# Output bias of the banded attention layers: from one-row products on TensorE to an addition into the residual on GpSimd

## The chip, the cores and the metric

The kernel runs on one core of a Trainium2 chip, in one launch. The metric is device time in microseconds. All times below come from hardware runs of it.

## The reference, cut to what matters

A first block (a token mixer with three branches, then a mixture of 16 experts) yields x, 256 tokens by 1024 features. Four post-norm transformer layers follow, and the change lies in two of them:

```python
for i in range(4):
    kind, j = i % 3, i // 3
    if kind == 0:   # layers 0 and 3: banded ("sliding window") attention
        h = mixer_a(x, a_w_qkv[j], a_b_qkv[j], a_sinks[j], a_w_o[j], a_b_o[j], cos, sin)
    elif kind == 1:
        h = mixer_b(x, b_w_qkv[j], b_w_o[j], cos, sin)
    else:
        h = mixer_c(x, c_w_qkv[j], c_w_o[j], cos, sin)
    x = layer_norm(DN_ALPHA * x + h, ln_g[i, 0], ln_b[i, 0])
    x = layer_norm(DN_ALPHA * x + swiglu(x, w_gate_up[i], w_down[i]), ln_g[i, 1], ln_b[i, 1])
```

`mixer_a` ends in `o.reshape(B, S, nq) @ w_o + b_o`: it alone has an output bias, `b_o`, one row of 1024 values that is the same for every token. DN_ALPHA is 8 to the power 1/4.

## The kernel before, in words

Each engine runs a program of its own; semaphores order them. Weights stream from HBM as units of 128x1024 values into a ring of 12 (SyncE's queue, L351). ScalarE rounds each unit into `high` (L1185), VectorE subtracts to get `low` (L1660), and every product of two fp32 operands is made of three: high by high, high by low, low by high. In the four layers all products run through the helper at L443. The residual x lies in SBUF as two tiles of 128 tokens by 1024; LayerNorm rewrites it in place (L2005, L2006), TensorE transposes it (`turn`, L531, counted in `x_turned`) and ScalarE and VectorE write its transposed halves `xs`, which the projections read.

A banded layer (`kind == 0`) treats its 16 heads as four quads q0 to q0+3. TensorE's order is written out by hand: projections of values, keys and the four quads' queries, the scores of each quad in between, then `weighted_values(q0)` and `weighted_values(q0+1)` (transposes of the weights at L1052 to L1054, then a gather into `pg`), then the output projection. ScalarE copies a gathered quad out as `oth` (L1559), VectorE subtracts for `otl` (L2215), counted in `otl_out`.

The output projection accumulates into the four banks of `pd`, one for each half of the features of each token tile. Before its first real product TensorE waits for `bo_landed` and opens each bank with a product of a row of ones by a row of the bias (L1131, both fp32, so each is recorded as two matmuls), and the last of them gives `bo_used`. `wo_part(n, t)` then adds the products with weight unit n: units 0 to 3 for both token tiles first, 48 products of 128x512 in all, behind `otl_out` of quad q0+1; then quad q0+2's values, units 4 and 5, quad q0+3's values, and the rest. VectorE's `residual(t, h)` reads a bank, computes ALPHA times x plus the bank in one instruction (L1966) and takes its statistics (L1970); LayerNorm follows, whose gain is `gb[:, 0]` and whose bias is `gb[:, 1]`.

GpSimd's queue, in the second half of the kernel, does two things. At the end of each LayerNorm it loads the rows for the next (L426 to L433), spread over all partitions: in front of a banded layer `a_bo` goes to `gb[:, 0]` (L428) and `ln_b` to `gb[:, 1]` (L429). `attention(layer)` then multiplies the exponentials of each quad by the reciprocals of their sums (`weigh`, L369), each behind VectorE's `recip`; between the third and the fourth quad of a banded layer it waits for `bo_used` and loads `ln_g` over the bias (L380). Nothing else is in its queue.

Of the kernel before, what the change touches and what calls it, by code (L numbers as in the profile page):

```python
# [22 lines left out]
ALU = mybir.AluOpType  # L23
# [4 lines left out]
KT = D // P  # L28
T = 256
TT = T // P  # L30
# [12 lines left out]
ALPHA = (2 * LAYERS) ** 0.25  # L43
# [74 lines left out]
def build_program(nc, a, out):  # L118
# [7 lines left out]
    with ExitStack() as ctx:  # L126
# [17 lines left out]
        ones = sb("ones", [P, P])  # L144
# [8 lines left out]
        gb = sb("gb", [P, 2, D])  # L153
# [45 lines left out]
        pd = pb("pd", [P, 4, 512])  # L199
# [14 lines left out]
        x = rs[:, 2048:4096].rearrange("p (t d) -> p t d", t=TT)  # L214
# [78 lines left out]
        def S(name):  # L293
            if name not in sems:
                sems[name] = ctx.enter_context(nc.semaphore(name))
            return sems[name]
# [24 lines left out]
        def row_of(name):  # L321

            o = D * LONG.index(name)
            return a["long_rows"][o:o + D].partition_broadcast(P)
# [35 lines left out]
        def _(gp):  # L360
# [12 lines left out]
            def attention(layer):  # L373

                kind, q0 = KINDS[layer], 4 * layer
                for i in range(3):
                    weigh(q0 + i)
                if kind == 0:
                    gp.wait_ge(S("bo_used"), layer // 3 + 1)
                    gp.dma_start(gb[:, 0, :], row_of(f"ln_g{2 * layer}")).then_inc(S("gains_landed"), 16)  # L380
                weigh(q0 + 3)

            gp.memset(cs[:, :, :], 0.0).then_inc(S("cs_zero"), 1)
# [40 lines left out]
            for n in range(3, 3 + 2 * LAYERS):  # L424
                layer = (n - 3) // 2
# [13 lines left out]
        def _(pe):  # L439
            held = [""]  # L440

            def mm(dst, lhs, rhs, start, stop, skip=False):
                ins = nc.tensor.matmul(dst, lhs, rhs, start=start, stop=stop, skip_group_check=skip)  # L443
                if held[0]:
                    ins.then_inc(S(held[0]), 1)
                    held[0] = ""
                return ins
# [131 lines left out]
            for k in range(KT):  # L579
                g = k % 4  # L580
                last = mm(pm[0][32 * g:32 * g + 32, :], wg32[:, k, :], hc[:, :, k, :], k < 4, k >= 4)
# [3 lines left out]
            for s in range(4):  # L585
                last = mm(pm[0][:, s * 16:(s + 1) * 16], gate_rows[:, s * P:(s + 1) * P], fold[:, 0:16], True, True)
# [7 lines left out]
            for r, dst in ((0, pm[1]), (1, pm[0])):  # L594
                for j in range(4):
                    fwd, bwd = (2, 3, 0, 1)[j], (3, 2, 1, 0)[j]
                    mm(dst[0:8, j * P:(j + 1) * P], zp[:, r, fwd, :], ident, True, False)
                    last = mm(dst[0:8, j * P:(j + 1) * P], zp[:, 2 + r, bwd, :], flip, False, True)
# [5 lines left out]
            for i in range(4):  # L604
                last = mm(pm[1][:, (4 + i) * 8:(5 + i) * 8], rr_of[(4, 0)[i // 2]][:, (2 + i % 2) * P:(3 + i % 2) * P],
                          ident[0:8, 0:8], True, True)
# [81 lines left out]
            for h in range(MLH):  # L688
                for t in range(2):
                    last = nc.tensor.transpose(pd[:, h // 2, (h % 2) * T + t * P:(h % 2) * T + (t + 1) * P],  # L690
                                               hml[:, t, h, :], ident)
# [386 lines left out]
            for layer, kind in enumerate(KINDS):  # L1078
# [45 lines left out]

                n0 = first[("wo", layer)]
                pe.wait_ge(S("masked"), PROJ[q0 + 4])
                if kind == 0:
                    pe.wait_ge(S("bo_landed"), 16 * (layer // 3 + 1))
                    for t in range(TT):
                        for c in range(2):  # L1130
                            last = mm(pd[:, 2 * t + c, :], ones[0:1, :], gb[0:1, 0, c * 512:(c + 1) * 512], True, False)  # L1131
                    last.then_inc(S("bo_used"), 1)

                def wo_part(n, t):
                    w = weights(n0 + n)
                    i, c = n // 2, n % 2
                    for k in (2 * i, 2 * i + 1):
                        for l, r in ((0, 0), (0, 1), (1, 0)):
                            o = (k % 2) * 512
                            last = mm(pd[:, 2 * t + c, :], (oth, otl)[l][:, k, t * P:(t + 1) * P], w[r][:, o:o + 512],  # L1140
                                      kind > 0 and k == 0 and (l, r) == (0, 0), k == KT - 1 and l == 1)
                    return last

                pe.wait_ge(S("otl_out"), q0 + 2)
# [483 lines left out]
        def _(dve):  # L1628
# [326 lines left out]
                then(V.tensor_tensor(mix[:, m, :], mix[:, m, :], mtmp[:, 0, :], ALU.add))  # L1955
                V.tensor_tensor(mix[:, m, :], mix[:, m, :], mtmp[:, 1, :], ALU.add).then_inc(S("mixed"), 1)

            def residual(t, h, mod=None):

                half = x[:, t, h * 512:(h + 1) * 512]  # L1960
                src = pd[:, 2 * t + h, :]
                if mod is not None:
                    then(V.tensor_tensor(rtmp, src, gb[:, mod, h * 512:(h + 1) * 512], ALU.mult))
                    ins = V.tensor_tensor(half, half, rtmp, ALU.add)
                else:
                    ins = V.scalar_tensor_tensor(half, half, ALPHA, src, ALU.mult, ALU.add)  # L1966
                ins.then_inc(S("res_out"), 1)
                RES[0] += 1
                dve.wait_ge(S("res_out"), RES[0])
                V.bn_stats(n_stats[:, t, h, :], half).then_inc(S("vector_step"), 1)  # L1970
                steps[0] += 1
# [247 lines left out]
            for layer, kind in enumerate(KINDS):  # L2219
# [72 lines left out]
                low_output(q0 + 3)  # L2292
                split_to(w0 + 11)
                n = 3 + 2 * layer
                for h in range(2):
                    dve.wait_ge(S("wo_first"), 2 * layer + h + 1)
                    residual(0, h)
                statistics(n, 0, False)
                normalised(n, 0)
                dve.wait_ge(S("unit_used"), w0 + 8 - split0)  # L2300
                residual(1, 0)
                low_part(n, 0)
                residual(1, 1)
                statistics(n, 1, False)
                normalised(n, 1)
                low_part(n, 1)
# [225 lines left out]
```

## Time and profile before

| | us |
|---|---|
| median of 3 runs (2242.11 to 2250.87) | 2242.16 |
| the profiled execution's own time | 2242.46 |
| its span, first to last instruction | 2240.6 |
| TensorE busy, matmuls | 2110.4 |
| VectorE busy | 1288.6 |
| ScalarE busy | 919.5 |
| GpSimd busy | 109.9 |

In the profile PE is TensorE's matmuls and PEld its weight loads, DVE is VectorE, ACT ScalarE, POOL GpSimd and SP SyncE. Durations in rows are us unless marked ns; a matmul's record is longer than its share of the array, since matmuls overlap, so the pace is read from the distance between two starts. In brackets stands how long the engine was idle before an instruction and what ended that. PEclk is the granted TensorE clock as a share of 2.4 GHz, so 0.50 is 1.2 GHz. Times along the run count from the first instruction. The profiled execution's time is 1.9 us more than its span.

### The profile page before, as it was taken

Reading aid. Unit: us, or ns where it says so; the run is one execution under the profiler, and the core shown is the slowest. Engines: PE = TensorE matmul, PEld = TensorE weight load, DVE = VectorE, ACT = ScalarE, POOL = GpSimd, SP = SyncE. Lnnn points to the kernel's source line nnn. Section 1 sums busy time; section 2 is a strip of 40 time slices with the busy share of each in tenths; the row PEclk is TensorE's granted clock in tenths of the full one; section 3 lists DMA queues with packets and bytes.
Section 4 is the critical chain, followed back from the end, with each engine's and each line's share of the span. In section 5 each row is a group of like instructions: output and inputs, shape, how many; then the busy total and the mean of one; then the engine's idle time right before and its main releaser. Section 6 shows DMA issues by size and latency. Waiting matters only on the chain.

```text
span 2240.6 us, 27821 instructions
## 1 busy us (share of the span) xinstructions
PE 2110.4 (94%) x11438; PEld 1691.7 (75%) x11438; DVE 1288.6 (58%) x1890; ACT 919.5 (41%) x1452; POOL 109.9 (5%) x115
## 2 busy tenths in 40 slices
PE   6999999998999988999999998999998999989997
PEld 2468667856888885788799997788796888867886
DVE  3345723346555575745677875755686655757554
ACT  2233341015444445444435554444364544454442
POOL 1000000000000002000001111000011000020000
PEclk9999999999999999999999999999999999989999
DMA  8142444434555541555453432555443555424541
GB/s 346 46 178 67 186 167 150 178 122 160 187 188 178 181 165 70 188 187 179 168 180 140 162 132 76 196 182 186 169 151 113 203 180 182 168 85 150 187 175 70
DMA packets 47118, 357.36 MB, mean 159 GB/s; under 512 B 5370, under 2 KB 5541, under 8 KB 9680
## 3 DMA queue, kind: packets, MB, share of 16 engines
q1 hardware_dynamic: 41904, 336.61, 41.4%
q0 software_dynamic: 4800, 18.50, 2.4%
q8 instruction: 91, 1.49, 0.3%
q10 hardware_dynamic: 288, 0.47, 0.1%
q14 instruction: 35, 0.29, 0.0%
HBM read 354.51 MB, written 1.05 MB: 159 GB/s over the span
## 4 chain that ended last, share of the span: by engine, by line
PE 85%; DVE 9%; ACT 4%; issue 1%; DMA 1%; POOL 0%; SPq 0%; ACTq 0%; DVEq 0%
PE pg L443 55%; PE pd L443 24%; PE pm L443 3%; PE pm L908 1%; DVE small L1970 1%; DVE rs L2006 1%; DVE rs L2005 1%; DVE rs L1966 1%; DMA ring<-in_wstream 1%; DVE low L1660 1%; PE pm L1052 1%; DVE ar L1764 1%; DVE xs L2016 1%; ACT high L1185 1%; ACT ar L1546 1%
## 5 line engine op out<-in xcount | busy, mean ns | idle before, releaser
L1660 DVE TENSOR_TENSOR low<-ring,high 128x1024 fp32r<-128x1024 f32 x512 | 619.8, 1231 | 372.3 <-ACT high L1185 372.0
L443 PE MATMUL pg<-high,xs 128*128 128x512 f32 (+1 forms) x2496 | 744.1, 375 | 24.1 <-DVE xs L2016 14.3
L1185 ACT CAST high<-ring 128x1024 fp32r<-128x1024 f32 x512 | 525.1, 1049 | 367.7 <-PE pd L443 164.5
L443 PEld LDWEIGHTS pg<-high,xs 128*128 128x128 f32 x2496 | 459.4, 192 | 112.9 <-issue 21.3
L443 PE MATMUL pg<-low,xs 128*128 128x512 f32 (+1 forms) x1248 | 465.0, 373 | 0.0
L443 PE MATMUL pd<-high,hid 128*128 128x512 f32 x960 | 311.9, 396 | 7.0 <-DVE hid L2095 7.0
L443 PEld LDWEIGHTS pg<-low,xs 128*128 128x128 f32 x1248 | 240.0, 192 | 40.5
L443 PE MATMUL pg<-xs,high 128*128 128x256 f32 x1344 | 242.1, 283 | 0.0
L443 PEld LDWEIGHTS pd<-high,hid 128*128 128x128 f32 x960 | 180.6, 188 | 50.9 <-DVE hid L2095 8.2
L443 PEld LDWEIGHTS pg<-xs,high 128*128 128x128 f32 x1344 | 206.2, 188 | 5.3 <-issue 5.0
L443 PE MATMUL pg<-rh,ring 128*128 128x256 f32 (+1 forms) x832 | 204.0, 405 | 0.0
L443 PEld LDWEIGHTS pg<-rh,ring 128*128 128x128 f32 x832 | 160.0, 194 | 42.4 <-issue 22.5
L443 PE MATMUL pd<-low,hid 128*128 128x512 f32 x480 | 189.7, 395 | 0.0
L443 PE MATMUL pg<-xs,low 128*128 128x256 f32 x672 | 189.3, 282 | 0.0
L443 PEld LDWEIGHTS pg<-xs,low 128*128 128x128 f32 x672 | 126.6, 188 | 0.0
L443 PEld LDWEIGHTS pd<-low,hid 128*128 128x128 f32 x480 | 90.3, 188 | 21.3
L369 POOL TENSOR_TENSOR ar<-ar,small 128x256 f32<-128x256 f32 (+1 forms) x64 | 83.7, 1336 | 409.5 <-DVE small L2208 409.5
L2095 DVE TENSOR_TENSOR hid<-pm,hid 128x512 fp32r<-128x512 f32 x60 | 41.4, 691 | 92.6 <-ACT hid L1477 92.6
L1477 ACT CAST hid<-pm 128x512 fp32r<-128x512 f32 x60 | 35.2, 587 | 124.4 <-PE pm L908 124.4
L1486 ACT ACTIVATE ar<-pg 128x256 f32<-128x256 f32 x120 | 46.0, 384 | 84.2 <-PE pg L443 84.1
L1546 ACT ACTIVATE ar<-ar,small 128x257 f32<-128x257 f32 (+5 forms) x128 | 66.9, 526 | 17.6 <-DVE small L2202 9.6
L1764 DVE SCALAR_TENSOR_TENSOR ar<-rs,vecs,ar 128x256 f32<-128x256 f32 x160 | 70.5, 482 | 2.9
(333 smaller groups left out, 1968.4 us busy)
## 6 DMA issues: line engine op xcount, KB each, us to landing
ring<-in_wstream SPq DMA_DIRECT2D x256, 1024.0 KB, 4.8
ring<-in_wstream SPq DMA_DIRECT2D x31, 2048.0 KB, 7.8
gb<-in_long_rows POOLq DMA_DIRECT2D x21, 512.0 KB, 4.5
hdec<-in_hy_decay POOLq DMA_DIRECT2D x4, 512.0 KB, 6.5
rh<-in_xt SPq DMA_DIRECT2D x1, 1024.0 KB, 11.7
rh<-in_ctx SPq DMA_DIRECT2D x1, 1024.0 KB, 20.0
cx<-in_cx_tables POOLq DMA_DIRECT2D x1, 1024.0 KB, 5.1
cx<-in_dft_tables POOLq DMA_DIRECT2D x1, 1024.0 KB, 8.5
```

Of the source, the lines that this page charges most:

```text
L369: last = gp.tensor_tensor(w, w, smx[:, b, 2, t, 2 * p:2 * p + 2].unsqueeze(2).to_broadcast([P, 2, n]), ALU.mult)
L443: ins = nc.tensor.matmul(dst, lhs, rhs, start=start, stop=stop, skip_group_check=skip)
L908: last = nc.tensor.transpose(pm[u % 2][:, i * T + t * P:i * T + (t + 1) * P], hidden[:, t, i * P:(i + 1) * P], ident)
L1052: nc.tensor.transpose(pm[i][:, 0:P], scores(q, 0)[:, h, g * P:(g + 1) * P], ident)
L1185: nc.scalar.copy(high[:, (s - split0) % NHIGH, :], ring[:, s % NRAW, :]).then_inc(S("high_done"), 1)
L1477: nc.scalar.copy(hid[:, u % 2, 0, :, :], pm[u % 2][:, :].rearrange("p (i t) -> p i t", t=T)).then_inc(S("hid_high"), 1)
L1486: nc.scalar.activation(silu_g[:, t, :], pg[t][:, 0:T], ACT.Silu).then_inc(S("silu_done"), 1)
L1546: last = nc.scalar.activation(s, s, ACT.Exp, bias=smx[:, b, 0, t, h:h + 1], accum_out=smx[:, b, 1, t, h:h + 1])
L1660: V.tensor_tensor(low[:, s % NRAW, :], ring[:, s % NRAW, :], high[:, (s - split0) % NHIGH, :].bitcast(F32), ALU.subtract).then_inc(S("low_ ...
L1764: last = V.scalar_tensor_tensor(d, src, w[i], d, ALU.mult, ALU.add)
L1966: ins = V.scalar_tensor_tensor(half, half, ALPHA, src, ALU.mult, ALU.add)
L2095: V.tensor_tensor(hid[:, u % 2, 1, :, :], pm[u % 2][:, :].rearrange("p (i t) -> p i t", t=T), hid[:, u % 2, 0, :, :].bitcast(F32), ALU.sub ...
```

## The change

In the two banded layers GpSimd waits until the bias has landed and x has been transposed, multiplies each tile of x by ALPHA, adds the bias row, and then loads `ln_g` over the bias. It does so ahead of the first quad's weighing. TensorE no longer opens the accumulators with one-row products, and the first real product of each bank overwrites it. VectorE waits for the additions and then adds the bank to x without a factor.

```diff
--- before.py
+++ after.py
@@ -373,11 +373,17 @@
             def attention(layer):
 
                 kind, q0 = KINDS[layer], 4 * layer
+                if kind == 0:
+                    gp.wait_ge(S("bo_landed"), 16 * (layer // 3 + 1))
+                    gp.wait_ge(S("x_turned"), 4 * (2 + 2 * layer))
+                    for t in range(TT):
+                        gp.tensor_scalar(x[:, t, :], x[:, t, :], ALPHA, None, ALU.mult).then_inc(S("x_raised"), 1)
+                        gp.wait_ge(S("x_raised"), 2 * (layer // 3) + t + 1)
+                        gp.tensor_tensor(x[:, t, :], x[:, t, :], gb[:, 0, :], ALU.add).then_inc(S("bo_added"), 1)
+                    gp.wait_ge(S("bo_added"), 2 * (layer // 3 + 1))
+                    gp.dma_start(gb[:, 0, :], row_of(f"ln_g{2 * layer}")).then_inc(S("gains_landed"), 16)
                 for i in range(3):
                     weigh(q0 + i)
-                if kind == 0:
-                    gp.wait_ge(S("bo_used"), layer // 3 + 1)
-                    gp.dma_start(gb[:, 0, :], row_of(f"ln_g{2 * layer}")).then_inc(S("gains_landed"), 16)
                 weigh(q0 + 3)
 
             gp.memset(cs[:, :, :], 0.0).then_inc(S("cs_zero"), 1)
@@ -1124,12 +1130,6 @@
 
                 n0 = first[("wo", layer)]
                 pe.wait_ge(S("masked"), PROJ[q0 + 4])
-                if kind == 0:
-                    pe.wait_ge(S("bo_landed"), 16 * (layer // 3 + 1))
-                    for t in range(TT):
-                        for c in range(2):
-                            last = mm(pd[:, 2 * t + c, :], ones[0:1, :], gb[0:1, 0, c * 512:(c + 1) * 512], True, False)
-                    last.then_inc(S("bo_used"), 1)
 
                 def wo_part(n, t):
                     w = weights(n0 + n)
@@ -1138,7 +1138,7 @@
                         for l, r in ((0, 0), (0, 1), (1, 0)):
                             o = (k % 2) * 512
                             last = mm(pd[:, 2 * t + c, :], (oth, otl)[l][:, k, t * P:(t + 1) * P], w[r][:, o:o + 512],
-                                      kind > 0 and k == 0 and (l, r) == (0, 0), k == KT - 1 and l == 1)
+                                      k == 0 and (l, r) == (0, 0), k == KT - 1 and l == 1)
                     return last
 
                 pe.wait_ge(S("otl_out"), q0 + 2)
@@ -1955,13 +1955,15 @@
                 then(V.tensor_tensor(mix[:, m, :], mix[:, m, :], mtmp[:, 0, :], ALU.add))
                 V.tensor_tensor(mix[:, m, :], mix[:, m, :], mtmp[:, 1, :], ALU.add).then_inc(S("mixed"), 1)
 
-            def residual(t, h, mod=None):
+            def residual(t, h, mod=None, raised=False):
 
                 half = x[:, t, h * 512:(h + 1) * 512]
                 src = pd[:, 2 * t + h, :]
                 if mod is not None:
                     then(V.tensor_tensor(rtmp, src, gb[:, mod, h * 512:(h + 1) * 512], ALU.mult))
                     ins = V.tensor_tensor(half, half, rtmp, ALU.add)
+                elif raised:
+                    ins = V.tensor_tensor(half, half, src, ALU.add)
                 else:
                     ins = V.scalar_tensor_tensor(half, half, ALPHA, src, ALU.mult, ALU.add)
                 ins.then_inc(S("res_out"), 1)
@@ -2292,15 +2294,17 @@
                 low_output(q0 + 3)
                 split_to(w0 + 11)
                 n = 3 + 2 * layer
+                if kind == 0:
+                    dve.wait_ge(S("bo_added"), 2 * (layer // 3 + 1))
                 for h in range(2):
                     dve.wait_ge(S("wo_first"), 2 * layer + h + 1)
-                    residual(0, h)
+                    residual(0, h, None, kind == 0)
                 statistics(n, 0, False)
                 normalised(n, 0)
                 dve.wait_ge(S("unit_used"), w0 + 8 - split0)
-                residual(1, 0)
+                residual(1, 0, None, kind == 0)
                 low_part(n, 0)
-                residual(1, 1)
+                residual(1, 1, None, kind == 0)
                 statistics(n, 1, False)
                 normalised(n, 1)
                 low_part(n, 1)
```

## Rows read from the trace of the kernel before

**Rows 1.** The page: busy time by engine; the chain that ended last.

```profile
PE 2110.4 (94%) x11438; PEld 1691.7 (75%) x11438; DVE 1288.6 (58%) x1890; ACT 919.5 (41%) x1452; POOL 109.9 (5%) x115
...
PE 85%; DVE 9%; ACT 4%; issue 1%; DMA 1%; POOL 0%; SPq 0%; ACTq 0%; DVEq 0%
```

**Rows 2.** Uses of tile gb, whole run: ns min/median/max; DMA issue to landing, us.

```profile
L443 PE MATMUL pd<-gb,ones x16: 587/1009/1218, 862.0 to 1996.3; 1*128 1x512 f32 x16
...
L1963 DVE TENSOR_TENSOR ar<-pd,gb x8: 674/688/692, 483.8 to 800.0; 128x512 f32<-128x512 f32 x8
...
L380 POOL DMA_DIRECT2D gb<-in_long_rows x2: 592/593/594, 866.4 to 1997.6; - x2
...
DMA to landing us min/median/max: 3.8/4.5/7.3
```

**Rows 3.** Timeline, 855 to 885 us, layer 0: start, duration in us, engine, line, operation.

```profile
862.03 4.07 PE L443 MATMUL pd<-gb,ones 1*128 1x512 f32 x8
...
862.77 0.69 DVE L2215 TENSOR_TENSOR otl<-pg,oth 128x512 fp32r<-128x512 f32 x1 [2.25 <-ACT oth L1559]
...
866.03 0.80 PE L443 MATMUL pd<-high,oth 128*128 128x512 f32 x1
...
873.05 0.40 PE L443 MATMUL pd<-high,oth 128*128 128x512 f32 x1
...
873.28 0.39 PE L443 MATMUL pd<-low,oth 128*128 128x512 f32 x1
...
879.99 0.27 PE L1052 MATMUL pm<-consts,ar 128*128 128x128 f32 x1
```

**Rows 4.** The chain that ended last, 880 to 890 us: start, duration in us, what.

```profile
884.14 0.70 DVE otl L2215
...
884.88 3.04 PE pd L443 x12
```

**Rows 5.** Timeline, 1980 to 2014 us, layer 3.

```profile
1990.12 7.19 PE L443 MATMUL pd<-gb,ones 1*128 1x512 f32 x8
...
1990.86 0.69 DVE L2215 TENSOR_TENSOR otl<-pg,oth 128x512 fp32r<-128x512 f32 x1 [3.72 <-ACT oth L1559]
...
1997.24 0.80 PE L443 MATMUL pd<-high,oth 128*128 128x512 f32 x1
...
2010.55 0.27 PE L1052 MATMUL pm<-consts,ar 128*128 128x128 f32 x1
```

**Rows 6.** Stretch, length, busy us of PE, PEld, DVE, ACT, POOL; PEclk, DMA, GB/s.

```profile
809.00:836.00 27.00, 27.00 (x243) 26.05 (x242) 20.82 (x29) 12.62 (x18) 0.00 (x0) 1.00 0.49 176
862.00:865.00 3.00, 3.00 (x9) 1.41 (x8) 2.23 (x3) 2.85 (x12) 1.13 (x2) 1.00 0.00 0
865.50:872.00 6.50, 6.50 (x15) 4.72 (x15) 0.49 (x3) 0.75 (x4) 3.76 (x5) 0.50 0.22 81
882.00:886.00 4.00, 2.59 (x21) 1.82 (x22) 1.61 (x2) 3.03 (x5) 0.00 (x0) 1.00 0.54 229
1985.50:1997.00 11.50, 11.08 (x30) 5.31 (x30) 4.86 (x9) 5.71 (x21) 3.17 (x4) 0.50 0.01 1
1997.00:2001.50 4.50, 4.50 (x11) 3.40 (x11) 0.00 (x0) 0.00 (x0) 3.76 (x5) 0.50 0.35 117
```

**Rows 7.** Timeline of GpSimd, 805 to 850 us; in brackets its idle time before.

```profile
841.97 3.98 POOL L369 TENSOR_TENSOR ar<-ar,small 128x256 f32<-128x256 f32 x4 [35.27 <-DVE small L2208]
```

**Rows 8.** GpSimd's instructions by form, whole run: busy us, mean ns of one.

```profile
L369 POOL TENSOR_TENSOR ar<-ar,small 128x1536 f32<-128x1536 f32 x8 | 24.8, 3102 | 0.0
...
L395 POOL MEMSET rs<- 128x3684 f32 x1 | 3.2, 3169 | 23.0 <-PE pd L443 23.0
```

**Rows 9.** VectorE's residual step, whole run: ns min/median/max.

```profile
L1966 DVE SCALAR_TENSOR_TENSOR rs<-rs,pd x32: 669/680/690, 895.1 to 2231.7; 128x512 f32<-128x512 f32 x32
```

**Rows 10.** Timeline of VectorE, 1965 to 1975 us, layer 3: the rotation's second step.

```profile
1969.66 1.25 DVE L2162 SCALAR_TENSOR_TENSOR ar<-ar,ropes 128x256 f32<-128x256 f32 x1
...
1973.82 0.42 DVE L2162 SCALAR_TENSOR_TENSOR ar<-ar,ropes 128x256 f32<-128x256 f32 x1
```

## The prediction, made before the changed kernel was run

> **What bounds the kernel now.** I read the page first, then every use of the bias rows, then the instructions in order of time around them in both banded layers, then the same stretches with TensorE's granted clock. The page says that TensorE is busy 94% of the span and carries 85% of the chain that ended last [rows 1]. So whatever leaves TensorE's queue without leaving a hole is worth its full duration. The rows on the bias then show 16 records of one-row products, two for each of the 4 accumulators of a layer, at 0.59 us in the one layer and about 1.0 us in the other [rows 2]. In order of time they are one block in each layer: in layer 0 from 862.03 to 866.03 us, where the first full product of the output projection starts [rows 3]; in layer 3 from 1990.12 to 1997.24 us [rows 5]. That is 4.0 and 7.1 us of TensorE for work that fills one row of the array.
>
> **What is late next.** The projection also waits for the low half of the second quad's output (`otl_out`), behind the same gather that TensorE has just finished. VectorE starts that subtraction at 862.77 us, 0.74 us after the block began [rows 3]. At a later hand-over of the same kind, where nothing covers it, TensorE starts 0.74 us after VectorE's start (884.14 to 884.88) [rows 4]. So without the block the first full product starts at 862.77 + 0.74 = 863.51 us, not at 862.03, and the block's removal gives 866.03 - 863.51 = 2.5 us. In layer 3 the same reckoning is 1990.86 + 0.74 = 1991.60, and 1997.24 - 1991.60 = 5.6 us [rows 5]. Together 8.1 us, out of 11.1 us of removed block; 3.0 us come back as an idle wait.
>
> **The clock.** In layer 0 the granted clock is 1.00 during the block (862 to 865) and 0.50, that is 1.2 instead of 2.4 GHz, in the 6.5 us behind it [rows 6]. TensorE was busy without a gap before that fall, and what it had been doing was the one-row block. The 48 full products that follow take 879.99 - 866.03 = 13.96 us, while two of them stand 0.23 us apart at the upper level (873.05, 873.28) [rows 3]; 48 x 0.23 = 11.0, so 2.9 us are lost to the lower level. In layer 3 the clock is 0.50 before and during the block and stays there for 4.5 us of full products behind it [rows 6]; the 48 products take 2010.55 - 1997.24 = 13.3 us [rows 5], a loss of 2.3 us, or 4.6 us of running at half speed.
>
> Would the clock hold in layer 0 after the change? TensorE would gather, idle 1.4 us and start full products. The hand-over of rows 4 is just that, and the stretch around it (882 to 886, TensorE busy 2.59 of 4.00 us) kept 1.00 [rows 6]. So I take the 2.9 us as gained, with bounds 0 and 2.9. In layer 3 the clock is low on arrival. Full products then start after 1.4 us of idling instead of after 7.1 us of one-row products; bounds are a gain of the whole 2.3 us and a loss of as much more; I take half of it gained, 1.1 us, since the trace shows the block unable to raise the clock in 7 us and full products able to in under 5 (those 4.6 us).
>
> The Trainium skill, TensorE: Matmul & The Clock Gate, section What's actually happening, ties the clock to how busy the array has been and does not discount thin products. By that rule the one-row block keeps the clock up and the new idle wait endangers it, so the sum would be 8.1 us or less. Here the trace disagrees: the clock fell under uninterrupted one-row products.
>
> **What is added on GpSimd.** Four passes over 128x1024 per layer: two multiplications by ALPHA, two additions of the bias, each behind its semaphore. The trace has no one-operand arithmetic there. Bounds per element come from the memset (3.17 us for 3684, 0.86 ns) and the widest product with a broadcast (3.10 us for 1536, 2.02 ns) [rows 8]: 0.9 and 2.1 us a pass, 6 to 8.3 us in all; I take 8, as the arithmetic is nearest to the second row. They wait for the bias to land, 4.5 us after its issue and at worst 7.3 [rows 2], and for the last transposes of x. GpSimd's queue is otherwise empty: its first weighing in layer 0 starts at 841.97 us after 35.3 us of idling, released by VectorE's reciprocal [rows 7]; layer 3 repeats this. So the passes run from about 810 to 818 us (813 to 821 at worst), 20 us before anything behind them is wanted. Cost 0; if that cover were gone, the 8 us would go straight into the weighing and the chain.
>
> The gain row (`ln_g`) is now loaded behind the passes at about 818 us, 48 us earlier than now (866.4 [rows 2]); it is one 512 KB transfer, beside weight loads that take half of the DMA time there (0.49 [rows 6]) and run a ring of twelve units ahead. It moves past all of GpSimd's weighing but no weight load waits behind it. Cost 0. GpSimd's fourth weighing no longer waits for `bo_used`; nobody waits for it at that time.
>
> **VectorE.** Its four residual steps per layer turn from a three-operand form (0.680 us) into a plain addition out of PSUM, for which 0.688 us is the nearest row [rows 2, 9]: 8 x 0.008, nothing. The added wait on `bo_added` is met by about 818 us, and the first residual comes behind 884 us. What may cost is sharing: with GpSimd at work the rotation's 128x256 step takes 1.25 instead of 0.42 us [rows 10]. From 809 to 836 us VectorE is busy 20.8 of 27.0 us and TensorE 27.0 of 27.0 [rows 6], so TensorE waits for none of it and VectorE can lose about 6.2 us. If it loses all 8 us of the passes, the excess is 1.8 us a layer. I take 0, because TensorE shows no gap at all there, so no split weight comes just in time.
>
> **Sum.** 2.5 + 2.9 in layer 0, 5.6 + 1.1 in layer 3, together 12.1 us. Everything behind layer 0 runs some 5 us earlier, and the stretches in which TensorE idles meet the clock's changes elsewhere; with the fall of layer 0 priced at 2.9 us, I set aside a quarter of another one, 0.8 us. The profiled execution took 2242.46 us (span 2240.6), 0.3 us over the median 2242.16; it gives 2231.2, and from the median 2242.16 - 11.3 = 2230.9 us.
>
> **Rivals.**
> 1. *The clock does not care what fills the array.* Then only 8.1 us are gained, and the new idle wait can cost another fall in one of the layers, 2.9 us: 2234 to 2237 us. For it: in layer 3 the clock was low before the block. Against it: the fall in layer 0. Chance 0.14; it is what that section's rule would do here.
> 2. *Falls elsewhere.* The block's price is regained but layers 1 to 3 pick up two more falls of about 2 us at the places where TensorE waits: 2235 us, chance 0.12. The opposite is as open: in layer 3, reached earlier, the clock may be up before the products start, as it is in layer 0 (1.00 at 862), which gives 1.2 us more there and spares the low stretch ahead of them, some 4 us in all: 2227 us, chance 0.17.
> 3. *VectorE starved, slower.* The passes on GpSimd run not 2 but 5 us each, and VectorE is held for their length. TensorE then waits for split weights: (20 - 6.2) x 2 = 27.6 us lost against 11.3 gained, 2258 us. It turns into a loss where a layer's passes hold VectorE for more than 6.2 + 5.7 = 12 us. For it: the threefold step of rows 10. Against it: the rates of rows 8. Chance 0.03. The Trainium skill, SBUF — State Buffer, section Who interferes with whom, states that a VectorE instruction with two SBUF inputs and a GpSimd one that reads SBUF block each other for a whole instruction, not by shares; by that rule the loss is at most the passes' own 8 us, 1.8 us a layer after the slack, and the time 2234.5. It speaks against this change, as the splits have two SBUF inputs; the threefold step agrees with it in kind.
> 4. *It does not do what it says.* TensorE, freed of the block, stands at another wait up to the old time: the transposes behind the 48 products, for instance, wait for ScalarE. 2242 us. ScalarE is busy 0.75 of 6.50 us behind the block [rows 6], so 0.03.
>
> The rest, 0.51, is the forecast with its own spread of about 2228.5 to 2233.5. A measurement here can tell about 0.5%, 11.2 us, from no change; the forecast sits on that line, so its cases split. Faster by more: rival 2's good side, 0.17, and a little over half of the forecast's 0.51, in all 0.45. Slower by more: rival 3 with a little for what I have not seen, 0.04. Within: the rest, 0.51. The range leaves out rivals 3 and 4 and the tails: 2226.5 to 2237.
>
> **What would show it.** No records of one-row products into these accumulators. The first full product about 0.74 us behind the start of VectorE's subtraction, with TensorE idle some 1.4 us before it. Granted clock 1.00 in the 48 products of layer 0, which then take 11.0 us. Four GpSimd passes of some 2 us from 4 to 5 us behind the bias's issue, over long before the first reciprocal. VectorE's first splits of the layer up to twice as long, and no new wait of TensorE's there. The forecast is wrong if TensorE's first product is later than that, if the clock falls under the projection in layer 0 as before, or if TensorE waits for a split weight in the first 27 us of a banded layer.

## The result, and the profile after

| | median, us | lowest to highest | runs |
|---|---|---|---|
| before | 2246.54 | 2242.11 to 2250.87 | 7 |
| after | 2234.39 | 2231.93 to 2238.45 | 7 |

The ratio is 0.9947, with a 95% interval from 0.9932 to 0.9963. The changed kernel is faster by 12.2 us where 11.3 were forecast (2242.16 to 2230.9, a ratio of 0.9950). The base moved: of the three runs known beforehand two are the lowest of the seven and one the highest, so that their median, 2242.16, lies 4.4 us under that of all seven. The changed kernel ran once more later, with 12 runs beside 23 of before: 2239.29 against 2248.64 us, 0.9953 [0.994, 0.9966].

The profiled execution of the changed kernel took 2233.47 us (span 2231.7). First the page: busy time by engine, to be held against [rows 1].

```profile
PE 2095.2 (94%) x11422; PEld 1688.4 (76%) x11422; DVE 1298.7 (58%) x1890; ACT 919.6 (41%) x1452; POOL 133.9 (6%) x123
```

TensorE has the 16 records of [rows 2] less and 15.2 us less work. GpSimd has 24.0 us more, VectorE 10.1 us more without one more instruction.

Next the chain that ended last, from the end of the gather to the end of the 48 products. The kernel before in layers 0 and 3 (two windows of the chain, one for each layer: start, duration, what):

```profile
859.50 2.61 PE pg L443 x16
862.10 18.05 PE pd L443 x56
...
1990.19 20.52 PE pd L443 x56
```

The changed kernel:

```profile
859.11 2.76 PE pg L449 x16
861.87 1.46 issue
863.33 12.71 PE pd L449 x48
...
1989.57 1.46 issue
1991.03 11.34 PE pd L449 x48
```

The 56 records (8 thin, 48 full) became an idle wait of 1.46 us and 48 full ones: 18.05 to 14.17 us in layer 0, 20.52 to 12.80 in layer 3, which is 3.9 and 7.7 us.

The wait is for `otl`, as forecast. The profile names no releaser for it ("issue"); the product starts 0.11 us behind the end of VectorE's subtraction, and in e3 below the wait is gone where the first products need only the quad before. The timeline of the changed kernel, VectorE's subtraction and TensorE's first full product in layer 0:

```profile
862.53 0.69 DVE L2217 TENSOR_TENSOR otl<-pg,oth 128x512 fp32r<-128x512 f32 x1 [3.78 <-ACT oth L1559]
...
863.33 0.77 PE L449 MATMUL pd<-high,oth 128*128 128x512 f32 x1 [1.46 <-issue]
```

The clock did not do in layer 0 what was forecast. Stretches of the changed kernel, with the columns of [rows 6] (busy us of PE, PEld, DVE, ACT, POOL; then PEclk, DMA, GB/s):

```profile
809.00:836.00 27.00, 27.00 (x262) 25.72 (x260) 23.69 (x28) 11.87 (x18) 10.32 (x5) 1.00 0.52 181
...
856.50:866.00 9.50, 6.95 (x28) 4.96 (x29) 5.30 (x9) 6.37 (x25) 3.51 (x5) 0.50 0.01 2
866.50:876.00 9.50, 9.50 (x44) 7.67 (x43) 0.00 (x0) 0.00 (x0) 2.34 (x3) 1.00 0.30 110
900.50:903.50 3.00, 3.00 (x8) 2.32 (x8) 2.52 (x9) 0.20 (x1) 0.00 (x0) 0.50 0.26 109
...
1991.00:2002.00 11.00, 10.97 (x48) 8.95 (x49) 2.46 (x4) 2.72 (x12) 3.18 (x4) 1.00 0.26 95
```

It was low (0.50) from before the gather until 866 us, through the new idle wait and the first full products, and 1.00 behind that. In layer 3 the clock was up for all 48 products. A low stretch (0.50 again) has appeared at 900.5 us, where the feed-forward products start. The kernel before at that place in layer 0, and in layer 3, where it has such a stretch too:

```profile
900.00:912.00 12.00, 9.26 (x46) 6.93 (x44) 10.75 (x21) 2.46 (x5) 0.95 (x2) 1.00 0.40 165
2036.00:2039.00 3.00, 3.00 (x9) 2.35 (x8) 2.49 (x9) 0.20 (x1) 0.00 (x0) 0.50 0.00 0
```

Last the passes on GpSimd, by the timeline, layer 0:

```profile
802.39 0.53 POOL L434 DMA_DIRECT2D gb<-in_long_rows  x1 [300.83 <-DVE rs L2005]
...
806.83 3.11 POOL L380 TENSOR_SCALAR rs<-rs 128x1024 f32<-128x1024 f32 x1 [3.39 <-DMA gb<-in_long_rows]
810.03 2.64 POOL L382 TENSOR_TENSOR rs<-rs,gb 128x1024 f32<-128x1024 f32 x1
812.64 3.74 POOL L380 TENSOR_SCALAR rs<-rs 128x1024 f32<-128x1024 f32 x1
816.47 2.41 POOL L382 TENSOR_TENSOR rs<-rs,gb 128x1024 f32<-128x1024 f32 x1
819.18 0.61 POOL L384 DMA_DIRECT2D gb<-in_long_rows  x1 [0.30 <-POOL rs L382]
840.21 3.98 POOL L369 TENSOR_TENSOR ar<-ar,small 128x256 f32<-128x256 f32 x4 [20.42 <-DVE small L2210]
```

They take 806.83 to 818.88, 12.1 us and not 8, and GpSimd then still idles for 20.4 us. VectorE pays for some of it; its timeline, 803 to 830 us (a line with x4 or x2 is that many splits together; two with nothing beside them take 2.35 us):

```profile
804.95 5.47 DVE L1660 TENSOR_TENSOR low<-ring,high 128x1024 fp32r<-128x1024 f32 x4 [0.22 <-ACT high L1185]
...
811.64 4.09 DVE L1660 TENSOR_TENSOR low<-ring,high 128x1024 fp32r<-128x1024 f32 x2 [1.22 <-ACT high L1185]
...
816.83 2.60 DVE L2163 TENSOR_TENSOR ar<-ar,ropes 128x512 f32<-128x512 f32 x1 [1.10 <-ACT ar L1529]
...
823.01 0.69 DVE L2163 TENSOR_TENSOR ar<-ar,ropes 128x512 f32<-128x512 f32 x1
```

Two splits took 4.09 us and a rotation step 2.60 instead of 0.69. TensorE is busy 27.00 of 27.00 us from 809 to 836 all the same.

### The profile page after: what moved, and what is told of

The parts are those of the page before. It is cut to its first block, busy times and chain, and to the rows that moved or that the text cites. A ratio compares the mean times of both kernels' runs of the same rounds, so it can differ in the third digit from the quotient of the medians.

```text
span 2231.7 us, 27799 instructions
## 1 busy us (share of the span) xinstructions
PE 2095.2 (94%) x11422; PEld 1688.4 (76%) x11422; DVE 1298.7 (58%) x1890; ACT 919.6 (41%) x1452; POOL 133.9 (6%) x123
## 4 chain that ended last, share of the span: by engine, by line
PE 85%; DVE 9%; ACT 3%; issue 2%; DMA 1%; POOL 0%; SPq 0%; ACTq 0%; DVEq 0%
PE pg L449 55%; PE pd L449 24%; PE pm L449 2%; PE pm L914 1%; DVE small L1972 1%; DVE rs L2008 1%; DMA ring<-in_wstream 1%; DVE rs L2007 1%; DVE low L1660 1%; PE pm L1058 1%; DVE ar L1764 1%; DVE rs L1968 1%; ACT high L1185 1%; ACT ar L1546 1%; DMA rh<-in_xt 1%
## 5 line engine op out<-in xcount | busy, mean ns | idle before, releaser
L1660 DVE TENSOR_TENSOR low<-ring,high 128x1024 fp32r<-128x1024 f32 x512 | 626.2, 1243 | 370.9 <-ACT high L1185 370.6
```

The costliest lines, as they stand in the source:

```text
L1660: V.tensor_tensor(low[:, s % NRAW, :], ring[:, s % NRAW, :], high[:, (s - split0) % NHIGH, :].bitcast(F32), ALU.subtract).then_inc(S("low_ ...
```

## The experiments

The theory: the gain is the one-row block taken off TensorE's path, part of it by its length and part by the clock, which thin products do not keep up; GpSimd's work costs nothing. The rivals: the gain is in the other edits (a plain addition, an earlier `ln_g`); the clock does not care what fills the array; the passes cost something that the gain hides.

Each ratio below is to the kernel before, measured beside it on the same chip; its interval in brackets is the 95% one. The chips differ, so ratios are compared and not microseconds. Stage times are from the chains that ended last.

### e1: the block gone, and no passes

```diff
-    gp.wait_ge(S("x_turned"), 4 * (2 + 2 * layer))
-    for t in range(TT):
-        gp.tensor_scalar(x[:, t, :], x[:, t, :], ALPHA, None, ALU.mult).then_inc(S("x_raised"), 1)
-        gp.wait_ge(S("x_raised"), 2 * (layer // 3) + t + 1)
-        gp.tensor_tensor(x[:, t, :], x[:, t, :], gb[:, 0, :], ALU.add).then_inc(S("bo_added"), 1)
-    gp.wait_ge(S("bo_added"), 2 * (layer // 3 + 1))
...
-    dve.wait_ge(S("bo_added"), 2 * (layer // 3 + 1))
...
-    residual(0, h, None, kind == 0)
+    residual(0, h)
...
```

The two other calls of `residual` change alike, and the output bias is left out of the result.

> The changed kernel without GpSimd's four passes in each banded layer; VectorE multiplies by ALPHA as before, and the output bias is left out of the result. Theory (the passes are hidden): the same time as the changed kernel, 2234 us within 2 us, TensorE's schedule in the first 27 us of a banded layer unchanged. Rival (VectorE's held splits cost something after all): 2 to 4 us faster than the changed kernel, 2230 to 2232.

Measured: 2238.24 us (5 runs) against 2248.72 (17): 0.9948 [0.9933, 0.9964]. The changed kernel has 0.9947 and 0.9953. So the four passes, the wait on `bo_added` and the plain addition cost nothing that can be measured; the intervals leave room for some 4 us either way, so by the times alone the rival of 2 to 4 us would not be excluded. The traces are sharper: TensorE's waits in front of the gather are the same with the passes and without (more under g1). The expected 2234 us were missed because the kernel before stood at 2248.7 on that chip; the ratio is the one expected.

### e2: the block back, for nothing

The changed kernel with the eight one-row products in front, on a row of other values; the first full products overwrite what they wrote.

```diff
     pe.wait_ge(S("masked"), PROJ[q0 + 4])
+    if kind == 0:
+        for t in range(TT):
+            for c in range(2):
+                mm(pd[:, 2 * t + c, :], ones[0:1, :], cxf[0:1, c * 512:(c + 1) * 512], True, True)
```

> The changed kernel with the eight one-row product records put back in front of the projection in each banded layer (their values are overwritten by the first real product). Theory (the block was the price, by its own length and by the clock falling under it): as slow as the kernel before, 2245 to 2248 us, with the granted clock at one half behind the block. Rival (only the block's length counts): 8 us above the changed kernel, 2242 us, and the clock behind the block no lower than without it. Rival (the gain came from elsewhere): 2234 us.

Measured: 2249.25 us (12 runs), 1.0002 [0.9989, 1.0015]. The block alone takes the whole gain away. Its chain, layer 0 and layer 3:

```profile
862.77 18.05 PE pd L449 x56
...
1994.97 16.89 PE pd L449 x56
```

Layer 0 takes the same 18.05 us as before to the last digit; layer 3 found a higher clock and lost 4.1 us against the changed kernel instead of 7.7. The eight records alone take 3.95 us there (1994.97 to 1998.92) where they took 7.1 in the trace of before: that figure was a matter of where the clock stood on arrival.

### c1 and c2: the block five times, thin and full

Both are made from the kernel before. c1 repeats the one-row products, c2 has the same count, columns and type with all 128 rows (the bias enters the result with another factor there).

c1:

```diff
+    for _ in range(4):
+        mm(pd[:, 2 * t + c, :], ones[0:1, :], gb[0:1, 0, c * 512:(c + 1) * 512], True, True)
     last = mm(pd[:, 2 * t + c, :], ones[0:1, :], gb[0:1, 0, c * 512:(c + 1) * 512], True, False)
```

c2:

```diff
-    last = mm(pd[:, 2 * t + c, :], ones[0:1, :], gb[0:1, 0, c * 512:(c + 1) * 512], True, False)
+    for _ in range(4):
+        mm(pd[:, 2 * t + c, :], ones[:, :], gb[:, 0, c * 512:(c + 1) * 512], True, True)
+    last = mm(pd[:, 2 * t + c, :], mean_w[:, :], gb[:, 0, c * 512:(c + 1) * 512], True, False)
```

> The kernel before with the block of one-row products issued five times over in each banded layer (40 records instead of 8). Theory (one-row products do not keep the clock up): the granted clock falls to one half inside the block and stays there to its end in both layers, wherever it began; a record then takes 0.85 us, the block some 28 to 34 us. Rival (a busy TensorE keeps its clock whatever fills the array): the clock rises within the block and stays, 0.43 us a record, 17 to 20 us.

> The same five-fold block with all 128 rows in each product (all rows of the bias tile are equal, so only the factor of the added bias changes, and the bias in the result is wrong). Theory: the clock is up within about 5 us of the block's start at the latest and stays there into the projection; 0.43 us a record at the upper level, 17 to 20 us a block, and 48 products of 11.0 us behind it. Rival: no difference from the one-row block.

Measured, one run each and so without an interval, before at 2245.66: c1 2299.71, c2 2264.9. That is 54 and 19 us for the same 64 extra records, 0.84 and 0.30 us each (in c2 the records themselves stand 0.41 us apart; the difference is what the other products of the stage gain). c1's chain and its stretches in layer 0:

```profile
864.33 2.76 PE pg L443 x16
867.09 43.89 PE pd L443 x88
```

```profile
867.50:870.00 2.50, 2.50 (x7) 1.10 (x6) 2.25 (x3) 2.50 (x12) 0.00 (x0) 1.00 0.00 0
871.00:898.00 27.00, 27.00 (x32) 9.99 (x30) 0.18 (x1) 0.23 (x2) 0.00 (x0) 0.50 0.00 0
898.00:901.00 3.00, 3.00 (x8) 2.35 (x8) 0.00 (x0) 0.00 (x0) 2.54 (x4) 0.50 0.39 142
902.00:910.00 8.00, 8.00 (x36) 6.49 (x35) 0.00 (x0) 0.00 (x0) 0.22 (x1) 1.00 0.36 132
```

The same of c2:

```profile
862.99 29.07 PE pd L443 x88
```

```profile
858.00:863.00 5.00, 4.28 (x23) 2.90 (x23) 1.89 (x5) 1.91 (x6) 3.17 (x4) 0.50 0.01 3
864.50:880.00 15.50, 15.50 (x38) 6.89 (x37) 2.38 (x4) 2.64 (x12) 0.00 (x0) 1.00 0.00 0
880.00:891.00 11.00, 11.00 (x48) 8.61 (x47) 0.00 (x0) 0.00 (x0) 3.77 (x5) 1.00 0.39 143
```

In c1 TensorE is busy without a gap (27.00 of 27.00 us) and the clock is down for all of it: it was 1.00 half a microsecond behind the block's start (867.5 to 870), 0.50 from 871 us on, and came back only once full products ran, which start at 898.1 us. In c2 the block starts inside a low stretch, the clock is up 1.3 us later (864.2) and stays up. Layer 3 of both runs does the same: 0.50 from 2028 to 2056 us under c1's block, 1.00 from 2007.8 to 2023 under c2's. Count, columns, type and busy share are alike; the rows are not. The Trainium skill, TensorE: Matmul & The Clock Gate, section What's actually happening, says that the clock follows how busy the engine has been. By that alone both blocks would hold it up; c1 shows that a busy engine is not enough when one row of the array is fed.

### e5: the block once, with full rows

The clock's share of the block's price without removing anything: before, with one line of the block changed (the bias again with another factor).

```diff
-    last = mm(pd[:, 2 * t + c, :], ones[0:1, :], gb[0:1, 0, c * 512:(c + 1) * 512], True, False)
+    last = mm(pd[:, 2 * t + c, :], mean_w[:, :], gb[:, 0, c * 512:(c + 1) * 512], True, False)
```

> The kernel before with its block unrepeated but with all 128 rows in each product (bias scaled wrongly in the result). Theory (part of the block's price is the clock): faster than before by 3 to 6 us, 2241 to 2243 us against 2247, with the products behind it at 11 to 13 us. Rival (only the length of the block counts): no change from before.

Measured: 2240.10 us (12 runs) against 2245.66 (23): 0.9971 [0.996, 0.9982], 6.5 us faster by the ratio, and the rival of no change falls. Eight records in each layer are there as before, and 0.29% has come in where the change itself brought 0.53 and 0.47%: more than half of it, though the intervals (0.18 to 0.40% here) would allow less. Its chain in layer 0, with 18.05 for the same 56 records before:

```profile
865.66 15.31 PE pd L443 x56
```

Two layers save 2.7 and 5.4 us in the stage (15.31 and 15.16 against 18.05 and 20.52). The 20.52 is what one trace of layer 3 shows (e2 has 16.89), but the products behind the block tell it without the block's own length: from the first to the next instruction behind them, the 48 took 11.5 us in each of the four layers behind full rows (e5, c2) and 12.8 to 14.0 us in each of the six behind one row (before, e2, c1).

### e3 and e4: fill the wait that is left

The 1.46 us of idling wait for quad q0+1, but the products with units 0 and 1 need only quad q0. e3 lets the first 24 start at once. e4 adds to it: for the second token tile, the 12 products with units 2 and 3 come behind the third quad's values, where TensorE would wait again.

```diff
-    pe.wait_ge(S("otl_out"), q0 + 2)
+    pe.wait_ge(S("otl_out"), q0 + 1)
     for n in range(4):
+        if n == 2:
+            pe.wait_ge(S("otl_out"), q0 + 2)
```

and e4 instead, with the first loop over units 0 and 1 alone:

```diff
+    pe.wait_ge(S("otl_out"), q0 + 2)
+    for n in (2, 3):
+        last = wo_part(n, 0)
+        if kind > 0:
+            wo_part(n, 1).then_inc(S("unit_used"), 1)
     if kind == 0:
         weighted_values(q0 + 2)
+        for n in (2, 3):
+            wo_part(n, 1).then_inc(S("unit_used"), 1)
```

> The changed kernel, with the first 24 full products of the projection, which read only the first quad, waiting for that quad's low half alone; the other 24 wait for the second quad's as before. Theory (the 1.46 us idle in front of the 48 products is a bare wait for VectorE's subtraction): that idle goes in both banded layers and the time falls by 2 to 3 us, to 2231 to 2232. Rival (TensorE reaches a later wait earlier and stands there): no change, 2234.

> As the early start, and in the banded layers the 12 products of units 2 and 3 for the second token tile stand behind the third quad's values, under the 1.37 us wait for that quad's low half. Theory (both waits are bare hand-overs): 2 x (1.46 + 1.37) = 5.7 us below the changed kernel, 2228 to 2230 us. Rival (units 2 and 3 are given back 3 us later and the ring or the split weights become late in front of the feed-forward part): the gain of the early start alone or less, 2232 or more.

Measured: e3 2231.21 us (6 runs), 0.9919 [0.9902, 0.9935]; e4 2229.89 (5), 0.9915 [0.9899, 0.993]. Both are faster than the changed kernel's 0.9947, e3 by more than the 2 to 3 us expected. Since the intervals overlap or touch, all three ran again side by side, before at 2248.64:

> The changed kernel once more, as a common yardstick for the three that run beside it. Expected ratio to the kernel before: 0.995, as at first. If it comes out at 0.992 or 0.993 instead, the first measurement was a little low and the early start is worth less than its first ratio says.

> The early start once more, beside the changed kernel on one chip. Theory (it removes two waits of 1.46 us and little else): 2.9 us or 0.13% below the changed kernel. Rival (the filled wait also keeps the clock up, as full products do): 5 to 6 us or 0.25% below it, with shorter stretches at half clock under the projection.

> Both waits covered, once more beside the changed kernel. Theory: 5.7 us or 0.25% below the changed kernel, and 2.7 us below the early start. Rival (the second cover only moves the wait): level with the early start.

Measured: the changed kernel 2239.29 (12 runs), 0.9953 [0.994, 0.9966]; e3 2229.29 (6), 0.9921 [0.9899, 0.9943]; e4 2230.37 (5), 0.9921 [0.99, 0.9942]. So e3 beats the changed kernel by 0.28 and 0.32%, 6.3 and 7.2 us, more than twice the 2.9 us of idling that it fills: the rival written down before its second run, and not the bare wait. The chain of e3's second run, layers 0 and 3:

```profile
864.36 11.81 PE pd L449 x48
...
1985.19 11.29 PE pd L449 x48
```

The products start at the gather's end, and take 11.81 us in layer 0 where the changed kernel took 12.71 and, in its second run, 12.77. With the wait the low stretch around the gather reached 2.8 to 3.4 us into the full products in eight layers of ten (after, its second run, e1, g1 and g2) and ended ahead of them in two; in e3's four it reached 1.4 us into them at most. The rest lies behind them: the low stretch in front of the feed-forward products (900.5 us above) is there in all ten of those layers and in none of e3's four. It costs 1.5 us (26.5 against 24.96 us from the first of those products to the first of the second half). From the first product of the second quad's gather to that point a banded layer took 67.3 us with the wait (after, its second run and e1) and 63.6 without, as means, 7.5 us for two layers: what the runs show. What decides whether the second low stretch falls is not shown: the kernel before and e2 have it in layer 3 and not in layer 0.

e4 filled the next wait too and cannot be told from e3, where 2.7 us more were expected. In layer 0 of both its traces the low stretch that costs 1.5 us has returned (63.2 and 64.0 us by the measure above, against e3's 63.8 and 64.0). In layer 3 it has not, and e4 is faster there, 61.6 against 63.3; that 1.7 us does not show in the medians, whose intervals are wider than it.

### g1 and g2: longer passes

The changed kernel with two (g1) or four (g2) more multiplications, by 1.0, for each tile of x. g1 is shown; g2 has 5 for 3.

```diff
+    for r in range(3):
+        gp.tensor_scalar(x[:, t, :], x[:, t, :], ALPHA if r == 0 else 1.0, None, ALU.mult).then_inc(S("x_raised"), 1)
+        gp.wait_ge(S("x_raised"), 3 * (2 * (layer // 3) + t) + r + 1)
```

> The changed kernel with each multiplication by ALPHA followed by four by 1.0, so that GpSimd's passes take about 3 x 10 + 2 x 3 = 36 to 38 us a layer instead of 12.4. Theory (there are 21 us of cover in front of the first weighing): passes end about 4 to 5 us after the first reciprocal, the weighing and TensorE's transposes start that much later, and 8 to 14 us are lost over both layers, with VectorE's held steps adding to it. Rival (VectorE's held steps decide long before the weighing does): TensorE waits for split weights or for rotated queries before 836 us of the run, and the loss is 20 us or more.

> The changed kernel with each multiplication by ALPHA followed by two by 1.0, GpSimd's passes then taking about 24 us a layer and ending near 834 us, before the first reciprocal. Theory (there is room for the passes as long as they end before the first weighing): level with the changed kernel. Rival, as the 38 us of passes suggested (VectorE, held at its shared steps, is late before the weighing is): 2 to 6 us slower than the changed kernel, VectorE's reciprocal later than 841 us of the run, and TensorE waiting for the rotated queries of the third quad longer than the 2.7 us of before.

Measured: g1 2245.60 us (10 runs), 0.9989 [0.9973, 1.0005], beside the changed kernel's 0.9953: 0.36% or 8.1 us lost. g2 2245.77 (10 runs), 1.0003 [0.9992, 1.0014]: the whole gain gone. The timeline of GpSimd in g1, layer 0:

```profile
832.89 2.64 POOL L383 TENSOR_TENSOR rs<-rs,gb 128x1024 f32<-128x1024 f32 x1
...
847.37 4.39 POOL L369 TENSOR_TENSOR ar<-ar,small 128x256 f32<-128x256 f32 x4 [10.93 <-DVE small L2211]
```

The passes are over at 835.5 and GpSimd idles for another 10.9 us until VectorE's reciprocal: GpSimd is not late, VectorE is, and the theory that there is room up to the first weighing fails. The waits of TensorE in g1, 806 to 855 us (in the changed kernel, and in the kernel before, the first is 2.7 and the second absent):

```profile
PE pd L450 <- DVE ar L2168: 4.0, 1, 4.0
PE pd L450 <- DVE ar L2185: 1.6, 1, 1.6
```

Layer 3 of g1 has the same two, so they add 5.7 of the 8.1 us. In g2 the first of them is 4.8 us in layer 0 and 8.4 in layer 3, and with the smaller waits for VectorE's `ar` beside them some 9 us are added in all. There GpSimd comes late as well (in layer 3 its first weighing starts at 1979.06, 3 us behind the reciprocal), but TensorE waits no longer for a weighing than before (1.5 us against 1.9 in layer 3).

The whole way says the same. From a banded layer's first product with the new x to the second quad's gather TensorE took 59.2 to 62.1 us in all 24 banded layers of the twelve traces other than g1 and g2, with the passes or without; 64.5 and 64.6 in g1; 64.7 and 67.7 in g2.

How long VectorE was held stands in its busy time, since its instructions are the same 1890 in all of them. The pages of e1 and g1, busy time by engine:

```profile
PE 2100.7 (94%) x11422; PEld 1688.3 (75%) x11422; DVE 1288.6 (58%) x1890; ACT 919.9 (41%) x1452; POOL 109.8 (5%) x115
```

```profile
PE 2103.5 (94%) x11422; PEld 1691.4 (75%) x11422; DVE 1305.3 (58%) x1890; ACT 919.9 (41%) x1452; POOL 157.7 (7%) x131
```

From e1's 1288.6 us it grows by 10.1 in the changed kernel, 16.7 in g1 and 18.9 in g2 (1307.5): 5.1, 8.4 and 9.5 us a layer. The first is under the slack of 6.2 us that the prediction read off [rows 6] and costs nothing, the other two are over it and cost 8.1 and some 11 us. The runs put the limit between 5.1 and 8.4 us; that it is 6.2 is an estimate from that one stretch.

## Why the prediction was right, point by point

**The block is the cause.** Shown: e2 gives back all of it, e1 keeps all of it. Rival 4 (it does not do what it says) falls.

**What is late next.** The forecast put the first full product 0.74 us behind VectorE's start; it came 0.80 us behind (862.53 to 863.33, 1990.23 to 1991.03), after 1.46 us of idling where 1.4 were forecast. The terms of 2.5 and 5.6 us for the block come out at 2.5 and 5.6: the block's 4.0 and 7.1 us less 1.5. They were the sound part of the sum for this trace, but the 5.6 holds a block at the lower clock: with the 3.95 us that e2's block took in layer 3, it would be 2.5.

**The clock, mis-sized in both layers.** For layer 0 the forecast took the whole 2.9 us; by the chain the 48 products went from 14.1 (866.03 to 880.15) to 12.7 us, 1.4 gained. The step that failed is the analogy with rows 4 and the stretch around them: there TensorE had idled with the clock up and it stayed up; here the clock was 0.50 in front of the gather and stayed so until 866 us, through the gather, the 1.46 us of idling and the first products. In the kernel before it was low in front of the gather too (0.50 from 859 to 861 us) and came up only just as the block began. The forecast had read the 1.00 at 862 us, not the stretch ahead of it, and took it as fixed. In layer 3 it took 1.1 of 2.3 us; the products went from 13.5 (1997.24 to 2010.71) to 11.3 us, 2.1 gained. The sign that the forecast named, 1.00 in the 48 products and 11.0 us for them, did not come in layer 0. The traces show that this term scatters: where the clock stands on arrival changed from run to run of one kernel (the changed kernel's second run took 12.77 and 12.91 us for the 48, e1 11.33 and 12.90). The sum of both layers came out better than either: 4.0 forecast, 3.5 measured in the profiled pair.

**The set-aside.** 0.8 us was kept for falls elsewhere. One came: 1.5 us in front of the feed-forward products of layer 0, where the profile of before has 1.00 (in layer 3 it has such a fall too). 11.6 us from the stage less 1.5 is 10.1; the spans differ by 8.9 (2240.6 and 2231.7), so another 1.2 us went elsewhere.

**GpSimd.** 8 us a layer were estimated, 12.1 measured; the one-operand multiplication takes 3.4 us as a mean and the addition 2.5, in the changed kernel's rows by form:

```profile
L380 POOL TENSOR_SCALAR rs<-rs 128x1024 f32<-128x1024 f32 x4 | 13.7, 3436 | 6.2 <-DMA gb<-in_long_rows 6.2
...
L382 POOL TENSOR_TENSOR rs<-rs,gb 128x1024 f32<-128x1024 f32 x4 | 10.1, 2536 | 0.3
```

The cost of 0 held (e1), but not for the reason given first. The 20 us ahead of the first weighing were called the cover, and g1 lost 8 us while it still had 10.9 of them left. The cover that ran out is the other one in the prediction, VectorE's slack, put at 6.2 us a layer, of which the passes took 5.1. No new wait of TensorE came in the first 27 us, as forecast. The worst case that all 8 us would fall on VectorE did not come: it is held for 5.1 of 12.1 us.

**Rival 3** (VectorE starved) is therefore what happens with longer passes: in g1 and g2 TensorE waits for VectorE's `ar`. What it waits for are rotated queries and masked scores (L2168 and L2185 in g1), not, as the rival had it, split weights. It was said to turn into a loss where the passes hold VectorE for 12 us a layer. g2 stands at that edge, 1.0003, with 9.5 us held: by the slack of 6.2, (9.5 - 6.2) x 2 = 6.6 us of holding stand against some 11 lost, of which some 9 are TensorE's longer waits. Why a held us costs more than itself was not tested. The Trainium skill, SBUF — State Buffer, section Who interferes with whom, has the two engines block each other for a whole instruction. The rotation's step of 2.60 us instead of 0.69 agrees: it ends 0.5 us behind the pass beside it (819.43 and 818.88).

**Rival 1** (the clock does not care what fills the array) is refuted by c1, c2 and e5, though its second half was half right: with the new wait the clock came up later and a low stretch of 1.5 us was added, and e3 without the wait has neither.

**Rival 2** (falls elsewhere) came in part on both sides: one fall more in front of the feed-forward products of layer 0, and in layer 3 the clock was up before the products started. In the changed kernel's second run it was not (12.91 us), so this side was chance.

**Luck.** Where the ratio is 0.9947 and 0.9950 was forecast, part of the agreement is luck. The forecast was built on one trace. Over all traces the stage (wait or block, and the 48 products) took 18.4 us as a mean of four layers with the one-row block (before, e2) and 13.8 of six without it (after, its second run, e1): 9.2 us for two layers where the sum had 12.1 and the profiled pair 11.6.

**VectorE's residual** stayed as it was; the tile's use in the changed kernel against [rows 9]:

```profile
L1966 DVE TENSOR_TENSOR rs<-rs,pd x8: 669/679/682, 891.0 to 2027.0; 128x512 f32<-128x512 f32 x8
```

**What stays open.** Over all those traces, the stretch from the first product of the second quad's gather to the feed-forward network's second half accounts for 7.6 us in two layers (71.1 against 67.3 us as means of four and six), while the medians differ by 12.2 and 9.4 us. Some 2 to 5 us are not placed. The profiled pair alone accounts for itself (10.0 us there, 8.9 in the spans). The record has a likely reason: both traces with the block come from fast executions of their kernels, before 2242.46 us where the median is 2246.54, and e2 2242.94, the fastest of its twelve, where it is 2249.25, while the three without it lie within 1.3 us of theirs. That the rest is such scatter of the clock was not shown.

## What to carry to other kernels

Count a bias product on TensorE by its path time at the clock it will leave behind: here a matmul over one row of the array was paid in full length, and the clock was down under it or under the full products that followed in all six layers that had it. Where such a product must stay, feeding all the rows with something harmless may be worth much of removing it (0.29% of some 0.5% here). Where one is removed, look at once for work that fills the wait that comes out, since here the idle 2.9 us were worth 6 to 7 (filling the next wait as well, in e4, gave nothing more). And when work goes to GpSimd beside a busy VectorE, budget it against VectorE's slack under TensorE, not against GpSimd's own idle time. Last, read a clock term from more than one trace before it goes into a sum: the same 48 products took 11.3 to 12.9 us in one kernel.

## What the runs showed of the hardware

- One-row fp32 products of 512 columns ran for 27 us without a gap at a granted clock of 0.50 (c1), and full-row ones in a block of the same count for 15.5 us at 1.00 (c2).
- GpSimd's multiplication by a constant over 128x1024 fp32 (3.11 to 3.74 us in layer 0) was slower than its addition of two such tiles (2.41 and 2.64), both beside a busy VectorE.
- The kernel before ranged from 2238.98 to 2255.04 us over 23 runs on one chip, 0.7%; with 12 runs of the changed kernel beside them the interval of the ratio was still 0.26% wide.
